# An attention layer's output projection: from two groups of token tiles to three, with four places for its split weight rows

## What is computed

```python
def _layer_out(x, oa, ga, ob, gb, gate, w_out, ln_g, ln_b):
    mixed = jnp.concatenate([oa * jax.nn.silu(ga), ob * jax.nn.silu(gb)], axis=-1)
    y = jnp.einsum('btm,md->btd', mixed, w_out)
    return _layer_norm(ALPHA * x + gate[:, None, :] * y, ln_g, ln_b)
```

## Time and profile before

| | us |
|---|---|
| median of 3 runs | 2170.78 |
| the profiled execution | 2169.62 |
| its span, first to last instruction | 2167.5 |
| TensorE busy in the span | 2003.6 (92%) |
| VectorE, ScalarE, GpSimd busy | 974.4, 705.0, 601.9 |
| chain that ended last: TensorE, VectorE, DMA | 75%, 10%, 4% |

### The profile page before, as it was taken

One profiled execution on the slowest core, in us unless ns is written; L12 is line 12 of the kernel. 1 busy time (PEld: TensorE's weight loads), 2 busy tenths in 40 slices (PEclk: granted clock), 3 DMA queues, 4 the chain that ended last, 5 costly groups with the idle time before them and its releaser, 6 DMA issues.

```text
span 2167.5 us, 34153 instructions
## 1 busy us (share of the span) xinstructions
PE 2003.6 (92%) x13111; PEld 1586.1 (73%) x13111; DVE 974.4 (45%) x2446; ACT 705.0 (33%) x1522; POOL 601.9 (28%) x607
## 2 busy tenths in 40 slices
PE   6889999959999999999899999999998889999991
PEld 3567789848888887888677777777776568777770
DVE  2433468876667776512223232232334422122447
ACT  2244422113233323333343434334435522221112
POOL 0331111112222222222222222222222434433333
PEclk8899999979999999999999999999999999999996
DMA  9943113312222222222211111111114134553443
GB/s 342 361 161 112 26 47 85 91 39 62 77 74 75 57 77 72 77 52 65 50 25 41 40 25 41 40 25 40 25 41 164 44 98 128 146 153 112 130 155 98
DMA packets 249922, 193.84 MB, mean 89 GB/s; under 512 B 149393, under 2 KB 202897, under 8 KB 247969
## 3 DMA queue, kind: packets, MB, share of 16 engines
q1 hardware_dynamic: 233072, 174.94, 28.2%
q10 hardware_dynamic: 15616, 12.49, 1.8%
q0 software_dynamic: 1072, 4.24, 0.6%
HBM read 171.28 MB, written 24.53 MB: 90 GB/s over the span
## 4 chain that ended last, share of the span: by engine, by line
PE 75%; DVE 10%; DMA 4%; ACT 4%; issue 3%; POOL 2%; SPq 1%; DVEq 0%; POOLq 0%; ACTq 0%
PE psum L1619 12%; PE psum L1621 10%; PE psum L1620 10%; PE psum L1697 6%; PE psum L1718 6%; PE psum L1719 5%; PE psum L1720 5%; PE psum L1655 5%; PE psum L1675 5%; DVE room L1202 4%; DVE room L1199 3%; DMA ada_ring<-in_w_ada_dram 2%; PE psum L1590 2%; PE psum L1546 2%; DMA w_raw<-in_w_out_dram 1%
## 5 line engine op out<-in xcount | busy, mean ns | idle before, releaser
L1619 PE MATMUL psum<-h_hi,w_hi 128*128 128x364 f32 (+1 forms) x1536 | 552.3, 360 | 6.7 <-issue 3.6
L1621 PE MATMUL psum<-h_lo,w_hi 128*128 128x364 f32 (+1 forms) x1536 | 507.2, 330 | 0.0
L1620 PE MATMUL psum<-h_hi,w_lo 128*128 128x364 f32 (+1 forms) x1536 | 504.2, 328 | 0.0
L1619 PEld LDWEIGHTS psum<-h_hi,w_hi 128*128 128x128 f32 x1536 | 290.3, 189 | 101.5 <-issue 96.1
L1081 POOL TENSOR_SCALAR room<-room 128x256 f32<-128x256 f32 (+9 forms) x252 | 149.0, 595 | 642.1 <-DVE room L1301 641.8
L1620 PEld LDWEIGHTS psum<-h_hi,w_lo 128*128 128x128 f32 x1536 | 292.2, 190 | 0.0
L1621 PEld LDWEIGHTS psum<-h_lo,w_hi 128*128 128x128 f32 x1536 | 290.3, 189 | 0.0
L1066 POOL TENSOR_TENSOR w_lo<-w_raw,w_hi 128x512 fp32r<-128x512 f32 x128 | 164.8, 1287 | 331.6 <-ACT w_hi L872 331.6
L1718 PE MATMUL psum<-w_hi,h_hi 128*64 128x512 f32 (+1 forms) x576 | 231.2, 401 | 14.1 <-POOL w_lo L1071 10.2
L1071 POOL TENSOR_TENSOR w_lo<-w_raw,w_hi 128x512 fp32r<-128x512 f32 x128 | 172.5, 1348 | 234.6 <-ACT w_hi L879 234.6
L1719 PE MATMUL psum<-w_lo,h_hi 128*64 128x512 f32 (+1 forms) x576 | 226.4, 393 | 0.0
(11 more groups left out here) (164 smaller groups left out, 2668.0 us busy)
## 6 DMA issues: line engine op xcount, KB each, us to landing
ada_ring<-in_w_ada_dram SPq DMA_DIRECT2D x64, 512.0 KB, 9.3
w_raw<-in_w_in_dram SPq DMA_DIRECT2D x256, 128.0 KB, 2.5
w_raw<-in_w_out_dram SPq DMA_DIRECT2D x256, 128.0 KB, 2.9
w_raw<-in_w_ada_dram SPq DMA_DIRECT2D x128, 128.0 KB, 2.1
x_rows<-in_x_prompt_dram SPq DMA_DIRECT2D x8, 1024.0 KB, 12.5
w_raw<-in_w_in_dram SPq DMA_DIRECT2D x32, 256.0 KB, 2.8
room<-in_x_prompt_dram SPq DMA_DIRECT2D x8, 1024.0 KB, 8.3
mix_transposed<-room SPq DMA_DIRECT2D x14, 544.0 KB, 3.0
```

Of the source, the lines that this page charges most:

```text
L1619: pe.matmul(Z, w_hi, hh[:, k, a:b], start=(k == 0), stop=False)
L1620: pe.matmul(Z, w_lo, hh[:, k, a:b], start=False, stop=False)
L1621: ins = pe.matmul(Z, w_hi, hl[:, k, a:b], start=False, stop=(k == KT - 1))
```

## The change

The nine tiles are three groups of three (`Y_GROUPS`, `YT = 3`), so there are 12 chunks and 192 weight rows; the matmuls are the same 1728. From row 16 on a split row has one of four places (`out_w`): two new ones, `w_hi_more` and `w_lo_more`, lie in the part of `room` that attention's probabilities, keys and values used. Rows 18 and 19 wait for the end of attention (`gated`), later ones for `row_used(q - 4)`. In attention's last body `out_parts` deals 3 parts for each row over the four slots, and row 0 no longer waits for `gated`. Groups 0 and 1 are normalised during the group that follows, two tiles in its second chunk and one in its third. In the last group ScalarE only takes the roots; VectorE normalises with the same two instructions as elsewhere, and neither ScalarE nor GpSimd touches the rows. `load_rest` loads three tiles' x, and the second gate only for the last group.

```diff
-Y_GROUPS = [range(0, 4), range(4, NTILE)]
+Y_GROUPS = [range(0, 3), range(3, 6), range(6, NTILE)]
 YC = 512
 YN = D // YC
 YK = YC // P
-Y_BASE = [0, YN * len(Y_GROUPS[0])]
+YT = 3
 Y_ORDER = [0, 1, 2, 7, 3, 4, 5, 6]
+OUT_SPLIT = 4
...
+def out_parts(step, s):
+
+    ks = OUT_FILL[step]
+    n = YT * len(ks)
+    return [(ks[w // YT], w % YT) for w in range(-(-n * s // 4), -(-n * (s + 1) // 4))]
...
+    s5 = ExitStack()
+    sb("before_more", [P, 9728], where=s5)
+    whi_more = sb("w_hi_more", [P, 2, 512], F32R, where=s5)
+    wlo_more = sb("w_lo_more", [P, 2, 512], F32R, where=s5)
+    s5.close()
     room = sb("room", [P, 13960])
...
-    y_first = of_room(0, 4 * D).rearrange("p (t n) -> p t n", t=4)
-    xres = of_room(8192, 5 * YC).rearrange("p (t n) -> p t n", t=5)
-    gatec = [of_room(10752 + YC * i, YC) for i in range(2)]
-    b_gate = of_room(11776, YC)
-    lnst = of_room(12288, 20).rearrange("p (t c) -> p t c", t=5)
-    eps = of_room(12308, 1)
-    bnst = ident[:, 0:5 * YN * 6].rearrange("p (t n) -> p t n", t=5)
+    y_first = of_room(0, YT * D).rearrange("p (t n) -> p t n", t=YT)
+    xres = of_room(6144, YT * YC).rearrange("p (t n) -> p t n", t=YT)
+    gatec = [of_room(7680 + YC * i, YC) for i in range(2)]
+    b_gate = of_room(8704, YC)
+    lnst = of_room(9216, 36).rearrange("p (g t c) -> p g t c", g=3, t=YT)
+    eps = of_room(9252, 1)
+    bnst = ident[:, 0:YT * YN * 6].rearrange("p (t n) -> p t n", t=YT)
...
-        return plain_h[:, :, P * i:P * i + P] if i < 4 else plain_l[:, :, 2 * P:3 * P]
+        t = YT * (g - 1) + i
+        return plain_h[:, :, P * t:P * t + P]
+
+    def out_w(q):
+
+        if q < KT:
+            return whi[:, q % SPLIT, :], wlo[:, q % SPLIT, :]
+        i = q % OUT_SPLIT
+        return (whi[:, i, :], wlo[:, i, :]) if i < SPLIT else (whi_more[:, i - SPLIT, :], wlo_more[:, i - SPLIT, :])
...
-            for w in range(g + 1):
+            for w in range(1 + g // 2):
...
-            if g:
+            if g == 2:
...
-        for c in range(1, 2 * YN):
+        for c in range(1, OUT_CHUNKS):
             g, n = c // YN, c % YN
             for k in range(2 if c == 1 else 0, KT):
                 load_out(KT * c + k)
                 if (c, k) == (YN, 4):
-                    sp.wait_ge(y_done.sem, y_done.at(Y_BASE[1]))
+                    sp.wait_ge(y_done.sem, y_done.at(y_tile(1, 0, 0)))
                     sp.dma_start(lng, row_of(io["ln_g"], 0, D)).then_inc(ln_loaded.sem, 16)
...
-            used, n = chunk_used(CHUNKS - 2 + q) if q < 2 else row_used(q - 2)
-            act.wait_ge(used.sem, n)
-            act.activation(whi[:, q % SPLIT, :], raw[:, s, :], ACT.Copy).then_inc(hi_ready.sem, 1)
+            if q in (KT + 2, KT + 3):
+                act.wait_ge(gated.sem, gated.at(UNITS))
+            else:
+                used, n = chunk_used(CHUNKS - 2 + q) if q < 2 else row_used(q - 2 if q < KT + 2 else q - OUT_SPLIT)
+                act.wait_ge(used.sem, n)
...
-                at_ = len(OUT_FILL[step]) * s
-                if OUT_FILL[step] and at_ % 4 == 0:
-                    hi_out(OUT_FILL[step][at_ // 4] + 1)
+                for k, i in out_parts(step, s):
+                    if i == 0:
...
+            g, n = c // YN, c % YN
+            if g and (n, k) == (0, 10):
+                act.wait_ge(ln_var.sem, ln_var.at(YT * g))
+                act.activation(lnst[:, g - 1, :, 2], lnst[:, g - 1, :, 1], ACT.Sqrt, bias=eps).then_inc(ln_std.sem, 1)
+            if g and (n, k) in ((2, 7), (2, 14), (3, 7)):
+                i = YT * (g - 1) + (k // 8 if n == 2 else 2)
                 act.wait_ge(ln_done.sem, ln_done.at(i + 1))
-                store_y(0, i)
...
-            act.wait_ge(ln_half.sem, ln_half.at(N0 + i + 1))
-            row = y_rows(1, i)[0:r]
-            act.activation(row, row, ACT.Identity, bias=lnst[0:r, i, 1:2], scale=lnst[0:r, i, 3:4]).then_inc(ln_hat.sem, 1)
-        for i in range(LAST):
...
+        for i in range(YT):
+            r = tile_rows(Y_GROUPS[2][i])
+            act.wait_ge(ln_var.sem, ln_var.at(2 * YT + i + 1))
+            act.activation(lnst[0:r, 2, i, 2:3], lnst[0:r, 2, i, 1:2], ACT.Sqrt, bias=eps[0:r]).then_inc(ln_std.sem, 1)
+        for i in range(YT):
+            act.wait_ge(ln_done.sem, ln_done.at(2 * YT + i + 1))
+            store_y(2, i)
...
-            pool.tensor_tensor(wlo[:, q % SPLIT, :], raw[:, s, :], whi[:, q % SPLIT, :].bitcast(F32), ALU.subtract).then_inc(lo_ready.sem, 1)
+            w_hi, w_lo = out_w(q)
+            pool.tensor_tensor(w_lo, raw[:, s, :], w_hi.bitcast(F32), ALU.subtract).then_inc(lo_ready.sem, 1)
...
-            pool.wait_ge(ln_hat.sem, ln_hat.at(i + 1))
-            pool.wait_ge(ln_scaled.sem, ln_scaled.at(i + 1))
-            row = y_rows(1, i)[0:r, 8:16, :]
-            pool.tensor_tensor(row, row, lnb[0:r, 8:16, :], ALU.add).then_inc(ln_pool.sem, 1)
...
+        def normalise(g, i):
+            t = YT * g + i
+            r = tile_rows(t)
...
+            row = y_rows(g, i)[0:r]
+            dve.scalar_tensor_tensor(row, row, lnst[0:r, g, i, 0:1], lng[0:r], ALU.subtract, ALU.mult).then_inc(ln_half.sem, 1)
+            dve.wait_ge(ln_half.sem, ln_half.at(t + 1))
+            dve.scalar_tensor_tensor(row, row, lnst[0:r, g, i, 3:4], lnb[0:r], ALU.mult, ALU.add).then_inc(ln_done.sem, 1)
...
-            dve.wait_ge(ln_hat.sem, ln_hat.at(i + 1))
-            dve.tensor_tensor(row[:, 8:16, :], row[:, 8:16, :], lng[0:r, 8:16, :], ALU.mult).then_inc(ln_scaled.sem, 1)
-            dve.tensor_tensor(row[:, 0:8, :], row[:, 0:8, :], lng[0:r, 0:8, :], ALU.mult).then_inc(dve_chain.sem, 1)
-            dve.wait_ge(dve_chain.sem, chained())
-            dve.tensor_tensor(row[:, 0:8, :], row[:, 0:8, :], lnb[0:r, 0:8, :], ALU.add).then_inc(ln_done.sem, 1)
...
+        for g in range(len(Y_GROUPS)):
+            for n in range(YN):
+                gates(g, n)
+                for i in range(YT):
+                    leave(g, n, i)
+                    if n == YN - 1:
+                        statistics(g, i)
+                if g and n == 0:
+                    dve.wait_ge(ln_std.sem, ln_std.at(g))
+                    dve.reciprocal(lnst[:, g - 1, :, 3], lnst[:, g - 1, :, 2]).then_inc(dve_chain.sem, 1)
+                    dve.wait_ge(dve_chain.sem, chained())
+                if g:
+                    for i in ((), (0, 1), (2,), ())[n]:
+                        normalise(g - 1, i)
+        for i in range(YT):
+            r = tile_rows(YT * 2 + i)
+            dve.wait_ge(ln_std.sem, ln_std.at(2 + i + 1))
+            dve.reciprocal(lnst[0:r, 2, i, 3:4], lnst[0:r, 2, i, 2:3]).then_inc(dve_chain.sem, 1)
             dve.wait_ge(dve_chain.sem, chained())
-            dve.tensor_scalar(lnst[0:r, i, 1:2], lnst[0:r, i, 0:1], lnst[0:r, i, 3:4], -1.0, ALU.mult, ALU.mult).then_inc(ln_half.sem, 1)
-        def affine(i):
-            r = tile_rows(Y_GROUPS[1][i])
-            row = y_rows(1, i)[0:r]
-            dve.wait_ge(ln_hat.sem, ln_hat.at(i + 1))
-            dve.tensor_tensor(row[:, 8:16, :], row[:, 8:16, :], lng[0:r, 8:16, :], ALU.mult).then_inc(ln_scaled.sem, 1)
-            dve.tensor_tensor(row[:, 0:8, :], row[:, 0:8, :], lng[0:r, 0:8, :], ALU.mult).then_inc(dve_chain.sem, 1)
-            dve.wait_ge(dve_chain.sem, chained())
-            dve.tensor_tensor(row[:, 0:8, :], row[:, 0:8, :], lnb[0:r, 0:8, :], ALU.add).then_inc(ln_done.sem, 1)
-        for n in range(YN):
-            gates(0, n)
-            for i in range(N0):
-                leave(0, n, i)
-        for i in range(N0):
-            statistics(0, i)
-        gates(1, 0)
-        for i in range(LAST):
-            leave(1, 0, i)
-        dve.wait_ge(ln_std.sem, ln_std.at(1))
-        dve.reciprocal(lnst[:, 0:4, 3], lnst[:, 0:4, 2]).then_inc(dve_chain.sem, 1)
-        dve.wait_ge(dve_chain.sem, chained())
-        for n in (1, 2):
-            gates(1, n)
-            for i in range(LAST):
-                leave(1, n, i)
-            normalise(2 * n - 2)
-            normalise(2 * n - 1)
-        gates(1, YN - 1)
-        for i in range(LAST):
-            leave(1, YN - 1, i)
-            statistics(1, i)
-            if i:
-                spread(i - 1)
-            if i >= 2:
-                affine(i - 2)
-        spread(LAST - 1)
-        for i in range(LAST - 2, LAST):
-            affine(i)
+            normalise(2, i)
...
-                if q == 0:
-                    pe.wait_ge(gated.sem, gated.at((PAIRS - 1) * STEPS - 1))
...
-                ks = OUT_FILL[u - STEPS * (PAIRS - 1)]
-                for w in range(len(ks) * s, len(ks) * s + len(ks)):
-                    out_part(ks[w // 4], w % 4)
+                for k, i in out_parts(u - STEPS * (PAIRS - 1), s):
+                    out_part(k, i)
...
-                    if (c, k, i) == (1, 0, 3):
+                    if (c, k, i) == (2, 0, 0):
                         pe.wait_ge(gated.sem, gated.at(UNITS))
```

66 lines of the change are left out of this document (22 added, 44 removed).

## The result

The changed kernel takes 2183.07 us, the median of 5 runs (2180.76 to 2184.54), the kernel before 2170.78 (2169.03 to 2174.48): a ratio of 1.0056, with a 95% interval of 1.0043 to 1.0068. Forecast were 2160.8 and a range up to 2176, so the time lies 22 us above the forecast, outside its range and on the other side of no change.

The account below looks back on a forecast made before the run. TensorE's matmuls were taken as the bound. Row 18 at 1764.1, plus stream 356.2, half clock 2.2 and stalls 10, gave 2132.5; the tail of 25 made span 2157.5, forecast as median 2160.8 us, range 2152 to 2176.

Parts of the forecast that it names:

- Attention's last body and the hole: End of attention: shorter slots give 5.3 us, fewer x bytes in the first load_rest 0.7; row 18 starts at 1764.1.
- The stream of matmuls: Projection from row 18 on: 174 rows of 9 matmuls at 0.2267 us, 0.2287 in group 2, 356.2 us.
- Half clock: TensorE at clock 0.50 behind the hole at attention's end, as in the kernel before: 2.2 us.
- Stalls: TensorE waiting for weight rows: bursts 3, gain and bias 4, stores 3, together 10 us, bounds 3 and 22.
- The one from gain and bias: Row 69: the layer norm's gain and bias, loaded behind row 68, stall TensorE about 4 us, between 3 and 6.
- the lead hides it: Third chunk: ScalarE waits for ln_done until about T + 12, TensorE wants row 8 at T + 16.4, so no stall.
- the two stores: Row 14 of third chunks, groups 1 and 2: a store in the burst costs 1.5 us each, 3 in all.
- back 7 rows after it was lost: Weight path: gaining 0.62 us a row with four split places, it regains the full 4.0 us lead in 7 rows.
- The tail: After the last matmul: three tiles left, normalised on VectorE alone, 25 us (bounds 24 and 29) where it was 46.8.
- (a): Rival at chunk starts: bursts still land in 12.3 us, each of ten stalls 1.5 us, 2173 us; chance 0.20.
- (b): Rival in the weight path: rows above 1.7 us instead of 1.43 don't regain the lead; 2190 us at 1.95; chance 0.13.
- (c): Rival in the tail: bound by stores with landings of 9.0 us, end 4 us later, 2165 us; chance 0.07.

Follow-up runs that it names:

- moved_places: Changed kernel with w_hi_more and w_lo_more 320 bytes further on, beginning at a multiple of 512 bytes: 2179.88 us, 1.0050 of the kernel before.
- clear_stores: Changed kernel with normalised groups' stores moved out of the third chunks, to rows 4 and 6 of the fourth and later: 2177.06 us, 1.0031.
- short_norm: Changed kernel with the two normalising instructions of groups 0 and 1 cut from 2048 columns to 128: 2168.54 us, 0.9991.
- spread_rest: Changed kernel with load_rest of chunks 1 to 11 in 256 KB pieces, one behind each of rows 9 to 14: 2164.91 us, 0.9981.
- all_moved: Changed kernel with the edits of moved_places, later_stores and spread_rest, and gain and bias in 16 pieces over two chunks: 2156.35 us, 0.9948.
- one_each: all_moved with the first three load_rests in later pieces and groups 0 and 1 normalised one tile in each of six chunks: 2146.24 us, 0.9894.
- each_bursts_clear: each_bursts with the stores at row 5 of the chunk after, the last at row 14 of the last chunk: 2157.82 us, 0.9944.
- each_old_place: one_each with the new places back at their old first byte, 64 bytes past a multiple of 128: 2148.98 us, 0.9908.
- place_steps: Changed kernel with w_hi_more moved 64 bytes, to a multiple of 256, and w_lo_more 192 bytes, to one of 128: 2183.36 us, 1.0062.
- each_bursts: one_each with load_rest again in one piece behind row 15 of each chunk, the first still in pieces: 2170.08 us, 1.0004.
- later_stores: Changed kernel with a normalised group's three stores moved to row 11 of the third chunk and rows 5 and 11 of the fourth: 2179.55 us, 1.0048.

## Why the prediction was wrong

Its sum ended 23.7 us too early: span 2157.5 instead of 2181.2. By its own steps:

- **Attention's last body and the hole**, predicted row 18 at 1764.1, measured 1768.28. 2.2 us of that are nothing of the change: the last body itself began that much later (a reciprocal of VectorE at 1661.65 in place of 1659.46). Of 6.0 us (5.3 and 0.7) 4.0 came. The slots got shorter, but TensorE then waited more for other engines, 16.9 us in the last body where it was 10.4. The lower bound (half of the slots count) had allowed for it.
- **The stream of matmuls**, 356.2 us predicted, 1566 x 0.2310 = 361.7 measured, 5.5 too few. I took the intervals of the earlier trace rows for operands that lie elsewhere, and moving them back alone gave 4.3 us of spacing (moved_places). Where an operand begins was in the diff (9728 elements ahead), and no step looked at it.
- **Half clock**, 2.2 predicted, 8.0 measured: 1.3 behind the hole, 1.6 behind row 69, 2.4 behind row 112 and 1.6 behind row 176. I priced it for the hole alone, and let it stand only as an upper end of the stall at row 69. These windows are of row 112, with a stall of 3.7 us (clock in the third column from the right; 0.50 is 1.2 GHz, 1.00 is 2.4):

```profile
1975.00:1978.00 3.00, 0.35 (x1) 0.35 (x2) 2.90 (x5) 1.98 (x4) 1.68 (x2) 0.76 0.46 133
1978.30:1983.00 4.70, 4.70 (x13) 3.68 (x12) 4.63 (x5) 0.88 (x2) 4.28 (x4) 0.50 0.57 153
1980.00:1990.00 10.00, 10.00 (x38) 8.00 (x37) 7.63 (x4) 2.53 (x4) 9.58 (x5) 0.83 0.44 115
```

- **Stalls**, 10 predicted, 16.6 measured. The one from gain and bias is as worked out: 4 predicted, 4.2 of idle time measured; its issues were at 1866.64 to 1869.52, and the next split waited 8.49 us for its load. Rows 104, 105, 168 and 169 took 4.1: the failed step is "the lead hides it". It counted ScalarE's wait against a full lead of 4 us and left out that GpSimd works at half its speed or less during exactly that time, though the earlier trace rows has a VectorE instruction slowed threefold beside GpSimd. Rows 112 and 176 took 6.1, predicted 3 for the two stores and next to nothing for the bursts. The bursts of groups 0 and 1 without a store cost what was said (0 at rows 32, 48, 64, 80, 96 and 128), those of group 2 without one 0.8 and 0.6. What stood at 112 and 176 was hardly the stores: with the stores away these two rows still had 6.0 us of gaps (clear_stores), with VectorE's long instructions away 1.4 (short_norm), with the bursts in pieces none (spread_rest).
- **The lead was spent several times.** This is the error behind the others. Each place of the third chunk was held against the same 4 us. One part took it at rows 101 to 105, and 4.7 us after row 105 the next one, burst and store, came. That the lead is "back 7 rows after it was lost" was worked out, but not laid beside the 7 rows from 105 to 112, in which the burst itself lies.
- **The tail**, 25 predicted, 26.4 measured. The first of the three tiles was done at 2153.45, but VectorE took it up at 2155.00 only, since the last burst, issued from 2143.55, had just landed: 1.5 us. Where that load lands before it is wanted, the tail is 24.9 (spread_rest, all_moved, one_each). The 2048-element instruction alone takes 2.35 us, 2.25 predicted; that is made up for elsewhere, since the 24.9 have it too (the timeline of VectorE in the tail, against the earlier trace rows):

```profile
2153.67 1.29 DVE L1385 TENSOR_TENSOR room<-room 128x512 f32<-128x512 f32 x2 [21.84 <-DMA room<-in_x_sample_dram]
2155.00 0.69 DVE L1396 TENSOR_TENSOR h_hi_plain<-psum,room 128x512 f32<-128x512 f32 x1
...
2161.92 0.10 DVE L1433 RECIPROCAL room<-room 128x1 f32<-128x1 f32 x1
2162.06 2.35 DVE L1412 SCALAR_TENSOR_TENSOR h_hi_plain<-h_hi_plain,room,h_lo_plain 128x2048 f32<-128x2048 f32 x1
2164.45 2.35 DVE L1414 SCALAR_TENSOR_TENSOR h_hi_plain<-h_hi_plain,room,h_lo_plain 128x2048 f32<-128x2048 f32 x1
...
2174.12 2.34 DVE L1414 SCALAR_TENSOR_TENSOR h_hi_plain<-h_hi_plain,room,h_lo_plain 64x2048 f32<-64x2048 f32 x1
```

The four sums, 4.2 + 5.5 + 5.8 + 6.6 for Te and 1.4 for the tail, make 23.5 of the 23.7.

**The rivals.** (a), slower bursts, would have given 2173, and its place was wrong: group 0 had no stall. Its "two of the four bursts" was a misreading: behind the hole the kernel before had three bursts in group 0, ahead of rows 32, 48 and 64, and the last two stalled. (b) had the right mechanism in part, that VectorE takes GpSimd's time; but it made it an average speed (a row takes more than 1.7 us everywhere), and the average of the subtraction is 1.43 to 1.50 us. It is the three or four subtractions at 2.7 to 3.1 us within one chunk that count. What stood against it, 1.43 us by the rows, came from rows of group 0, where VectorE has no long instruction. (c) didn't happen: the stores of the tail landed in time.

**Turns between the queues.** The Trainium skill, "DMA: Bandwidth & Descriptors", section "Queues, rings and completion order", says that a DMA engine takes turns between the queues that have work. The prediction worked out 3.3 us for each of two stores by that rule, and took 1.5. From row 96 on, taking the stores away from the bursts took 3.0 us of gaps and half clock away for two stores (clear_stores, which also took ScalarE's wait out of the third chunks) and 5.6 for five (each_bursts_clear): at most 1.5 and 1.1 us each. So the value I took was the right size, the full price of the rule was not what the stream paid, and no run here shows the turns themselves.

## What to carry over

Write down a lead as an account in time: what it is at each row, what each transfer, wait and slowed instruction takes, and when it is back. Several charges within one recovery are one sum against one lead, not each against a full one. The same bytes in pieces between the rows they compete with, the same long instructions one pair at a time, stores apart from bursts, and first bytes at a multiple of 512 brought 35 to 37 us here with no work removed. And try the parts of a change alone: the layer norm on VectorE alone beat the kernel before, the whole did not.

## What the runs showed of the hardware

- Matmuls of 128x512 fp32r whose moving operands begin 64 bytes past a multiple of 128 in their partition follow one another after 0.233 us (means of whole rows: 0.2331 in the changed kernel, 0.2332 in each_old_place), at a multiple of 512 after 0.228 (0.2280 in moved_places, 0.2282 in one_each). With two of three at a multiple of 256 and the third at one of 128 it is 0.2300 (place_steps).
- GpSimd's subtraction of 128x512 takes 1.29 us alone and 2.7 to 3.1 beside VectorE's two-operand instructions over 2048 elements, which themselves take 2.35 alone and up to 3.4 beside it (the changed kernel, third chunks of groups 1 and 2).
- 1.25 MB issued in three transfers ahead of a row cost the stream 0 to 0.7 us at rows 48 to 96 of each_bursts, and 1.6 and 1.9 at rows 112 and 128, where a store of 1 MB from another queue went out 3.4 to 5.3 us before and a tile was normalised in the chunk. The same bytes in pieces of 256 KB behind each of five rows cost nothing (one_each).
- Behind a stall of 3.7 us in the changed kernel TensorE's granted clock was 0.50 (1.2 GHz) from 1978.30 to 1983.00 and then 1.00 (2.4 GHz). The length of a stall alone doesn't tell: behind 1.8 us at row 176 of each_bursts_clear it read 0.65 over the next 3.8 us, behind 3.1 us at row 69 of later_stores 1.00.
